# Attention steps: where a step's filler matmuls stand against its transposes

## What is computed

```
# first block, for each of 2 layers (L = 528 tokens kept: 16 meta + 512)
y_a = causal_block_attention(a_q, a_k, a_v, 64 ** -0.5, log_cum)   # 8 heads, forget gate
y_b = causal_block_attention(q_b, k_b, v_b, 96 ** -0.5)            # 8 heads of 64 + 32
y_c = sliding_window_sink_attention(qc, kc, vc, sinks)             # 8 heads of 64, window 128
# second block, layer 0 and layer 1
ao = diff_attention(...)        # 4 heads, two maps each
bo = dilated_attention(...)     # 8 heads
o  = mixer_c: for each query block, top-k keys by an index score, then 16 heads of 96
# each map
s = q @ k.T * scale ; s = where(mask, s, NEG) ; p = softmax(s) ; o = p @ v
```

## Time and profile before

| what | us |
|---|---|
| median of 3 runs | 2764.42 (2761.56 to 2770.17) |
| span of the profiled execution | 2763.7 |
| PE busy in it | 2667.6 (97%) |
| DVE busy | 1553.8 (56%) |
| ACT busy | 1139.5 (41%) |
| POOL busy | 129.8 (5%) |

### The profile page before, as it was taken

How to read it: one execution, slowest core, us unless ns; L and a number is a source line. 1 busy time by engine, 2 the same in 40 slices (tenths; PEclk the granted TensorE clock), 3 DMA queues, 4 the chain that set the end, 5 groups by cost and what they waited for, 6 DMA issues and landing times. The chain is left out here.

```text
span 2763.7 us, 40735 instructions
## 1 busy us (share of the span) xinstructions
PE 2667.6 (97%) x15744; PEld 2216.9 (80%) x15744; DVE 1553.8 (56%) x3335; ACT 1139.5 (41%) x2522; POOL 129.8 (5%) x140
## 2 busy tenths in 40 slices
PE   8999999999999999999999999999998899999998
PEld 7879979899988877878877677888786657788887
DVE  5365656655546555655678463443567875533446
ACT  3345332543333443343435553332355564432333
POOL 1001000000100100000013000000003300000000
PEclk9999999999999999999999999999999899999999
DMA  3201212222220221223321122232231102232333
GB/s 131 83 26 56 63 37 86 58 73 85 88 81 28 67 58 55 84 62 94 96 85 56 43 84 88 95 97 96 88 93 44 48 1 77 85 99 95 96 95 96
DMA packets 115265, 205.33 MB, mean 74 GB/s; under 512 B 13824, under 2 KB 23680, under 8 KB 114944
## 3 DMA queue, kind: packets, MB, share of 16 engines
q1 hardware_dynamic: 114064, 200.14, 23.7%
q10 hardware_dynamic: 1008, 2.59, 0.3%
HBM read 200.51 MB, written 2.10 MB: 73 GB/s over the span
## 5 line engine op out<-in xcount | busy, mean ns | idle before, releaser
L2348 PE MATMUL pp<-Hh,wh 128*128 128x512 f32 (+1 forms) x2336 | 865.6, 371 | 34.4 <-DVE Hl L1892 15.6
L2350 PE MATMUL pp<-Hh,wl 128*128 128x512 f32 (+1 forms) x2336 | 806.0, 345 | 0.0
L2349 PE MATMUL pp<-Hl,wh 128*128 128x512 f32 (+1 forms) x2336 | 806.0, 345 | 0.0
L1861 DVE TENSOR_TENSOR wl<-raw,wh 128x512 fp32r<-128x512 f32 (+2 forms) x738 | 481.7, 677 | 411.9 <-ACT wh L1660 400.9
L1660 ACT ACTIVATE wh<-raw 128x512 fp32r<-128x512 f32 (+2 forms) x774 | 451.4, 605 | 352.9 <-PE pp L2350 292.4
L2348 PEld LDWEIGHTS pp<-Hh,wh 128*128 128x128 f32 x2336 | 446.9, 191 | 122.1 <-issue 23.2
L2349 PEld LDWEIGHTS pp<-Hl,wh 128*128 128x128 f32 x2336 | 447.8, 192 | 55.3 <-issue 6.2
L2350 PEld LDWEIGHTS pp<-Hh,wl 128*128 128x128 f32 x2336 | 446.4, 191 | 52.4
L2348 PE MATMUL pp<-Yh,wh 128*128 128x512 f32 (+1 forms) x1222 | 453.5, 371 | 3.0 <-DVE wl L1861 1.8
L2350 PE MATMUL pp<-Yh,wl 128*128 128x512 f32 (+1 forms) x1222 | 435.8, 357 | 0.0
L2349 PE MATMUL pp<-Yl,wh 128*128 128x512 f32 (+1 forms) x1222 | 435.7, 357 | 0.0
(11 more groups left out here) (279 smaller groups left out, 2806.0 us busy)
## 6 DMA issues: line engine op xcount, KB each, us to landing
raw<-in_w SPq DMA_DIRECT2D x698, 256.0 KB, 2.6
raw<-in_w SPq DMA_DIRECT2D x36, 192.0 KB, 2.4
raw<-in_w SPq DMA_DIRECT2D x40, 128.0 KB, 2.0
out<-X SPq DMA_DIRECT2D x8, 256.0 KB, 2.0
con<-in_con SPq DMA_DIRECT2D x1, 1513.0 KB, 6.6
X<-in_x SPq DMA_DIRECT2D x2, 528.0 KB, 6.0
X<-in_x ACTq DMA_DIRECT2D x2, 528.0 KB, 6.8
Z<-in_p ACTq DMA_DIRECT2D x2, 512.0 KB, 3.2
```

The lines of the kernel that those rows point to most:

```text
L1861: e.tensor_tensor(part("wl", j), landing(j), part("wh", j).bitcast(F), ALU.subtract).then_inc(*dve.up("split", j))
L2348: e.matmul(it.ps, wh, xh, start=it.first, stop=False)
L2349: e.matmul(it.ps, wh, xl, start=False, stop=False)
L2350: e.matmul(it.ps, wl, xh, start=False, stop=it.end).then_inc(*pe.up())
```

## The change

The first of the two calls of `fill()` moves down: from between the scores and the transposes to behind the issue of the exponentials, beside the second one. The number of calls, of filler steps and of all instructions is the same; PE has 12408 rows in either order.

```diff
                 heads[-1]["exp"] = heads[-1]["mix"](heads[-1])
-            fill()
             if len(pend1) > (deep if u else 0):
                 turn(pend1[0])
                 pend2.append(pend1.pop(0))
             for v in new:
                 exp(v)
+            fill()
             fill()
             if len(pend2) > (1 if u else 0):
                 product(pend2.pop(0))
```

## The result

The changed kernel takes 2794.64 us (median of 4 runs, 2791.6 to 2794.91), against 2762.99 us before (4 runs, 2760.8 to 2770.17). The ratio is 1.0102, with a 95% interval of 1.009 to 1.0115: slower by 25 to 32 us. The forecast was 2772, the range ended at 2788. The direction was right; the measured loss is more than three times the 7.7 us of the forecast and lies beyond the range.

What follows compares the result with a forecast made beforehand. PE, busy 97% of 2763.7 us, was taken to bound the kernel. Terms -2.5 + 2.5 + 5.4 + 2.4 - 1.8 + 1.7 = +7.7 us on the median 2764.4 gave 2772 us, range 2757 to 2788.

Steps and rivals of the forecast that it cites:

- the line on the queues of DVE and ACT: DVE, ACT, POOL and SP queues: splits issued a few tenths of a us later, two panels ahead of use; 0 us.
- Neighbours on PE: 50 steps with filler between 64-row scores and transposes: transposes right behind the scores pay 0.05 us less each; -2.5 us.
- Waits for the 16 extra scores: 528-key steps, transposes (L2410) waiting for DVE's L2097: six old waits lose filler cover, +2.5 us; seven new ones, +7.0.
- The one wait of the scores for the bank's copy: Split and late copy of bank 5 held the next scores 1.58 us; this wait goes away, -1.6 us.
- The waits of transposes for copies: Transposes waiting for the previous unit's copy or for exponentials: some eight lose filler ahead; half counted, +2.4 us, between 0 and 4.8.
- Spread: Spread's waits for the copy out of bank 5, 5.2 us in six places, shrink; -1.8 us, between -5.2 and 0.
- Clock: PE's granted clock: one more stretch at the lower level after some seven more waits; +1.7 us, between 0 and 5.
- the two signs that the prediction gave for being wrong: L2410 doesn't wait more often, or idle time rises most in the second block, where only 2.4 us was put.
- much slower: Rival: waits at L2410 in 14 steps at up to 1.7 us, three more clock drops; +23 us, 2787 us; chance 0.22.

## Why the prediction was wrong

The step that failed is the line on the queues of DVE and ACT: "Splits are issued a few tenths of a us later in a step ... 0." In every fourth step of two attentions they are issued behind a copy that waits for PE's product at the end of the step, and DVE stands idle ahead of it for 1.8 to 4.6 us. The prediction named what stands behind the moved copy (gate, split, L2097) and priced it by steps in which the copy was free to go. It never asked what that copy itself waits for besides its transposes. Both facts were in the kernel (four map buffers, products for four), and the idle time of 3.01 us ahead of a DVE copy stood in the trace of before. What stands behind such a queue had no term either, above all the wait for L2139. Without the blocked copy (products for two) the move costs 1.7 us in these attentions instead of 16.6, so some 15 of the 28 us hang on it. The queues don't make this loss alone: by the stretches, it needs PE's new order for the larger part. The prediction took the filler's cover away only where PE waits for L2097, a copy or exponentials.

A second step was missing: what PE's filler waits for. The evacuation of a filler group moves behind copy and exponentials too, and with two banks PE feels it. The last attention lost 5.3 us; in its trace the waits for evacuations rose by 2.9 (0.5 to 3.4) and those for ACT's copy by 1.9.

Term by term:

- Neighbours on PE, -2.5. The prediction's own figures give 0.20 - 0.16 = 0.04 us each, so -2.0 for 50 places. The price for one is right: behind 64-row scores that end at 1563.81, the first transpose now ends at 1564.08, 0.27 later.

```profile
1563.11 0.70 PE L2403 MATMUL pp<-K,Q 64*128 64x256 f32 x4
1563.75 0.33 PE L2415 MATMUL pp<-con,Q 128*128 128x128 f32 x1
```

- Waits for the 16 extra scores, +2.5 and +7.0: the mechanism is right, the size is not. They went from 6.0 in 6 places to 9.5 in 9, not to 15. The six old waits stayed as they were (6.3 in sum, not 8.5). The split now stands between the copy out of bank 5 and L2097 in 14 steps instead of 7, as said, but only 2 of the 7 new ones make PE wait, 2.7 us in all, not 7.0. The last 0.5 is at an old place that had no wait before. The one wait of the scores for the bank's copy went, as said (1.6).
- The waits of transposes for copies, +2.4: measured +5.3 (13.9 to 19.2).
- Spread, -1.8: measured -3.8.
- The read of the spread, L2139: not in the sum, measured +9.6 (3.9 to 13.5).
- Clock, +1.7: nothing in the net, since PE's busy time is the same and the mean granted clock is 0.984 before and 0.985 after. It moved. In layer 1's second attention, two stretches ran at the lower level, where there was none before. One began after a wait of 1.88 us, the other in the wait of 4.09:

```profile
1031.60:1035.00 3.40, 3.40 (x10) 2.62 (x9) 0.80 (x2) 1.10 (x3) 0.00 (x0) 0.50 0.22 75
1065.90:1072.60 6.70, 5.24 (x14) 3.71 (x15) 3.05 (x8) 1.64 (x4) 0.00 (x0) 0.50 0.11 40
```

They explain the 4.7 us of busy time there, and other stretches had as much less. Whether that was luck can't be said from one profile each.

Neither of the two signs that the prediction gave for being wrong came true: L2410 does wait more often for L2097 (9 times instead of 6), and more of the loss lies in the first block (16.6 + 3.9) than in the second (8.3). The 8.3 is still over three times the 2.4 that it had put there. The rival "much slower" came nearest in size, by another cause (+23, extra scores and clock).

## What to carry to other kernels

When work is moved past an instruction in an in-order queue, price the wait of that instruction at its worst step, not its mean: list all that it waits for, rings of buffers above all, and look for the idle time ahead of it in the trace, even on an engine that is half idle. In this kernel the cover on the busy engine was worth most where another engine came late out of such a wait, and a block's end, where buffers, a shared bank and the output come together, held 11.6 of the 16.6 us; it is the place to look first. And see what frees the banks of the filler itself.

## What was not expected of the hardware

Nothing in the single durations: L1861 took 0.69 us, L2124 0.69, L2139 0.69 and L1660 0.61 in either kernel at 512 columns. New was that the losses of the parts added up, over nine attentions that follow each other on one core: 28.8 us by parts, 28.2 for the whole. That they agree to 0.6 us is luck, with parts known to 3 or 4 us.
